# The residual of the first output projection in chunks, the third feed-forward product read early, and the first transposes of prompt attention between its scores

## What is computed

```python
yp = yp + jnp.concatenate([mix_p, att_p], axis=-1) @ w_out[i]
f_p, c_p = conv_ffn(rmsnorm(yp, g_ffn[i]), zeros, w_up[i], conv_w[i], conv_b[i], w_down[i])

def conv_ffn(h, prev, w_up, conv_w, conv_b, w_down):
    u = h @ w_up
    ext = jnp.concatenate([prev, u], axis=1)
    y = conv_b + sum(conv_w[k] * ext[:, k:k + l] for k in range(CONV_WIDTH))
    a, v = jnp.split(y, 2, axis=-1)
    return (jax.nn.silu(a) * v) @ w_down, ext[:, -(CONV_WIDTH - 1):]
```

## Time and profile before

| | us |
|---|---|
| median of 3 runs | 3093.95 (3091.4 to 3095.31) |
| the profiled execution, its own time | 3097.18 |
| its span, first to last instruction | 3095.1 |
| mean granted TensorE clock | 0.975 of full |
| PE busy in the span | 2953.5 |

### The profile page before, as it was taken

One profiled execution on the slowest core, in us unless ns is written; L12 is line 12 of the kernel. 1 busy time (PEld: TensorE's weight loads), 2 busy tenths in 40 slices (PEclk: granted clock), 3 DMA queues, 4 the chain that ended last, 5 costly groups with the idle time before them and its releaser, 6 DMA issues. The chain is left out here.

```text
span 3095.1 us, 51036 instructions
## 1 busy us (share of the span) xinstructions
PE 2953.5 (95%) x19316; PEld 2727.1 (88%) x19316; DVE 1572.5 (51%) x3486; ACT 814.9 (26%) x1506; POOL 954.3 (31%) x420
## 2 busy tenths in 40 slices
PE   8998979999989999999999999899999999999998
PEld 7996956666667799999999999897899999999998
DVE  6212147777545516652643726396247626526262
ACT  5002026767633303320211202114123202102020
POOL 4430000000000133444444443460344444444443
PEclk9999979999989999999999999999999999999999
DMA  6117730000257331111111111313111111111112
GB/s 185 52 40 241 248 141 2 1 2 1 77 162 229 99 113 46 41 38 51 41 41 48 38 51 38 117 53 118 41 53 35 40 48 47 38 51 36 52 36 89
DMA packets 128571, 222.76 MB, mean 72 GB/s; under 512 B 16006, under 2 KB 92140, under 8 KB 127232
## 3 DMA queue, kind: packets, MB, share of 16 engines
q1 hardware_dynamic: 108436, 201.57, 20.0%
q10 hardware_dynamic: 19980, 19.14, 2.3%
HBM read 202.61 MB, written 22.18 MB: 73 GB/s over the span
## 5 line engine op out<-in xcount | busy, mean ns | idle before, releaser
L382 POOL TENSOR_SCALAR weights_high<-weights_whole 128x1024 fp32r<-128x1024 f32 (+2 forms) x168 | 434.7, 2588 | 1065.9 <-PE banks L417 894.1
L413 PE MATMUL banks<-ffn_in_high,weights_high 128*128 128x364 f32 (+1 forms) x2112 | 468.5, 330 | 16.9 <-DVE ffn_in_low L280 9.2
L415 PE MATMUL banks<-ffn_in_low,weights_high 128*128 128x364 f32 (+1 forms) x2112 | 468.2, 330 | 0.0
L417 PE MATMUL banks<-ffn_in_high,weights_low 128*128 128x364 f32 (+1 forms) x2112 | 466.6, 329 | 0.0
L413 PEld LDWEIGHTS banks<-ffn_in_high,weights_high 128*128 128x128 f32 x2112 | 367.3, 189 | 18.9 <-issue 18.9
L2749 DVE SCALAR_TENSOR_TENSOR conv_out<-conv_ext,conv_w,conv_out 128x1024 f32<-128x1024 f32 x176 | 322.0, 1829 | 109.7 <-ACT conv_out L2685 94.9
L384 POOL TENSOR_TENSOR weights_low<-weights_whole,weights_high 128x1024 fp32r<-128x1024 f32 (+2 forms) x168 | 367.2, 2186 | 24.7 <-issue 0.2
L417 PEld LDWEIGHTS banks<-ffn_in_high,weights_low 128*128 128x128 f32 x2112 | 368.8, 189 | 0.0
L415 PEld LDWEIGHTS banks<-ffn_in_low,weights_high 128*128 128x128 f32 x2112 | 368.4, 189 | 0.0
L2777 DVE TENSOR_TENSOR x<-x,banks 128x728 f32 (+1 forms) x128 | 86.5, 718 | 386.9 <-PE banks L417 386.9
L2685 ACT ACTIVATE conv_out<-conv_ext,conv_b,conv_w 128x1024 f32<-128x1024 f32 (+1 forms) x176 | 138.3, 834 | 542.6 <-DVEq L2740 542.4
(11 more groups left out here) (431 smaller groups left out, 4618.7 us busy)
## 6 DMA issues: line engine op xcount, KB each, us to landing
weights_whole<-in_w_up SPq DMA_DIRECT2D x88, 512.0 KB, 3.5
past_rows<-in_kv_pages SPq DMA_DIRECT2D x160, 128.0 KB, 2.3
z<-in_kv_pages SPq DMA_DIRECT2D x96, 128.0 KB, 2.4
weights_whole<-in_w_down SPq DMA_DIRECT2D x32, 384.0 KB, 3.1
weights_whole<-in_w_down SPq DMA_DIRECT2D x32, 320.0 KB, 2.9
x<-in_cmp_pages ACTq DMA_DIRECT2D x64, 128.0 KB, 5.8
x<-in_cmp_pages SPq DMA_DIRECT2D x64, 128.0 KB, 5.6
cmp_rows<-in_cmp_pages ACTq DMA_DIRECT2D x64, 128.0 KB, 5.3
```

Of the source, the lines that this page charges most:

```text
L382: pool.tensor_scalar(high, whole, 1.0, None, ALU.mult)
L413: pe.matmul(o, wh, high[:, at], start=kk == 0, stop=False)
L415: pe.matmul(o, wh, low[:, at], start=False, stop=False)
L417: last = pe.matmul(o, wl, high[:, at], start=False, stop=kk == len(terms) - 1)
```

## The change

Three edits, and the order of the instructions behind them.

1. `project`, only where there is a residual to load: each of the eight chunks has a semaphore and a transfer of its own (546 KB). SP issues chunks 0 and 1 when each is split, then weight tiles 2 and 3, then chunks 2 to 7, then the other tiles. DVE waits for chunk m before it takes product m, and its loop is written out.
2. `conv_ffn`: DVE takes product 2 (gate half of pair 1) right after the taps of the gate half of pair 0. Pair 1 is written out too, so that the loop of the first part starts at pair 2.
3. `prompt_attention`: the last three score phases of period 1 move behind the first transposes, and the scores of period 2 close up behind them; DVE weighs units 0 and 1 one after the other ahead of these phases; ACT's exponentials of units 3 and 4 start with the fifth copy instead of the first.

```diff
--- before.py
+++ after.py
@@ -431,21 +431,28 @@ project
-        late_loaded = k.sem(ctx, "late_loaded")
+        late_loaded = [k.sem(ctx, f"late_loaded{m}") for m in range(n)] if late_load else []
...
-            def late():
-                if late_load:
-                    tokens.wait_ready(sp)
-                    sp.dma_start(late_load[0][:], late_load[1].rearrange("k p t -> p k t")).then_inc(late_loaded, 16)
-            if w.fetched:
-                late()
+            def late(first, end):
+                for m in range(first, end):
+                    tokens.wait_chunk(sp, m)
+                    sp.dma_start(late_load[0][:, m, :], late_load[1][m]).then_inc(late_loaded[m], 16)
+            if late_load:
+                late(0, 2)
+                for s in range(2):
+                    w.load(sp, 2 + s, s, w_src[2 + s], cols)
+                late(2, n)
+                with sp.Fori(2, n // 2) as j:
+                    for s in range(2):
+                        w.load(sp, j * 2 + s, s, w_src[j * 2 + s], cols)
+            elif w.fetched:
                 rest_of_pairs(sp, n, lambda m, j, s: w.load(sp, m, s, w_src[m], cols), w.fetched)
...
@@ -483,13 +490,16 @@ project, VectorE
-            if late_load:
-                dve.wait_ge(late_loaded, 16)
...
-            pairs(dve, n, take)
+            if late_load:
+                for m in range(n):
+                    dve.wait_ge(late_loaded[m], 16)
+                    take(m, m // 2, m % 2)
+            else:
+                pairs(dve, n, take)
@@ -1212,6 +1223,9 @@ prompt_attention (AHEAD = 3)
         starts = [0] + [2 * ((ends[2 * p + 1] - 1) // 2) - 1 for p in range(NP)]
+        for f in range(AHEAD, PHASES):
+            places.setdefault(f - AHEAD, []).append((1, f))
+        starts[0] = PHASES - AHEAD
         for p in range(NP - 2):
@@ -1303,9 +1317,8 @@ prompt_attention, TensorE
-            for p in range(2):
-                for f in range(PHASES):
-                    score(p, f)
+            for p, f in [(0, f) for f in range(PHASES)] + [(1, f) for f in range(AHEAD)]:
+                score(p, f)
@@ -1420,12 +1433,12 @@ prompt_attention, VectorE
-            for f in range(3):
+            for f in range(AHEAD):
                 phase(1, f)
-            weigh(0)
-            for f in range(3, PHASES):
+            for u in range(2):
+                weigh(u)
+            for f in range(AHEAD, PHASES):
                 phase(1, f)
-            weigh(1)
@@ -1501,7 +1514,9 @@ prompt_attention, ScalarE
-                    for x in range(total * r // count, total * (r + 1) // count):
+                    later = 0 if p else 4
+                    first, end = (total * max(0, y - later) // (count - later) for y in (r, r + 1))
+                    for x in range(first, end):
                         ahead[x // STEPS](x % STEPS)
@@ -2724,18 +2739,22 @@ conv_ffn, VectorE
+            def take(t, av):
+                w.wait_product(dve, t)
+                for dst, src, r in pieces(av):
+                    last = dve.tensor_tensor(dst, src, r, ALU.mult)
+                last.then_inc(taken, 1)
+
             def convolve(p, m, base):
-                first = p == 0 and isinstance(m, int)
+                first = p == 0 and isinstance(m, int) and m == 0
+                second = p == 0 and isinstance(m, int) and m == 1
...
-                    if not first:
-                        w.wait_product(dve, m * 2 + (base + av))
-                        for dst, src, r in pieces(av):
-                            last = dve.tensor_tensor(dst, src, r, ALU.mult)
-                        last.then_inc(taken, 1)
+                    if not first and not (second and av == 0):
+                        take(m * 2 + (base + av), av)
...
                     if av == 0:
                         last.then_inc(convolved, 1)
+                        if first:
+                            take(base + 2, 0)
...
-            convolve(0, 0, 0)
-            finish(0, 0)
+            for m in range(2):
+                convolve(0, m, 0)
+                finish(0, m)
             for p, n in enumerate(PARTS):
-                with dve.Fori(1, n) as m:
+                with dve.Fori(1 if p else 2, n) as m:
```

3 lines of the change are left out of this document (2 added, 1 removed).

## The result

| | before | with the change |
|---|---|---|
| median, first comparison | 3090.18 (3082.21 to 3095.31, 6 runs) | 3066.9 (3061.91 to 3071.37, 6 runs) |
| median, second comparison | 3090.07 (3086.36 to 3097.34, 23 runs) | 3070.66 (3063.22 to 3076.54, 6 runs) |
| the profiled execution | 3097.18, span 3095.1 | 3065.29, span 3063.1 |
| mean granted TensorE clock in it | 0.975 | 0.982 |

The change makes the kernel faster: the ratio is 0.992, 95% interval 0.9901 to 0.9939, and 0.9932 (0.9918 to 0.9945) the second time, thus 19 to 23 us. The forecast was 3074.4 with a range from 3068 to 3085: the sign and the places were right, the time was 1.1 us under the range in the first comparison and inside it in the second. The two profiled spans differ by 32.0 us, more than the comparisons give, so a part of that difference is not the change; the stages tell which.

A forecast was written before the change was run, and what follows sets the result against it. TensorE, busy 2953.5 of 3095.1 us, was taken as the bound. Projection 8.5, feed-forwards 8.6 and attention 2.5 sum to 19.6 us, taken from the median 3093.95: forecast 3074.4, range 3068 to 3085.

The forecast's parts named there:

- Bound, places, order: Whole kernel: TensorE bounds it, stalls at four places can go, and PE's earlier start there is an earlier end.
- Projection: First output projection: PE's 5.6 us wait for weight tile 2 and 2.9 us of low clock go, gain 8.5.
- The margin of tile 2: Projection: tile 2 lands about 2 us before it is needed, its split ends 6.7 us before PE wants it.
- Feed-forward: Fifth product of each layer: stall of 5.6 us removed, 1.3 comes back, net gain 4.3 a layer, 8.6 for both.
- But product 5 needs product 3 read: Feed-forward: PE waits at worst 1.6 us at product 5; 0.8 counted, plus 0.5 for clock and product 6.
- a loop's entry: Feed-forward: the first state copy took 1.88 us instead of 0.17 on entering the loop; writing out pair 1 might remove it.
- its gate half is as late as before and no later: Feed-forward, pair 1: it begins with the state copy instead of the reads, so its gate half keeps its lateness.
- the stall's 5.6 us: Feed-forward, fifth product: 4.04 us lost around the wait plus 1.6 in slow groups after it, for each layer.
- Attention: Start of prompt attention: the transposes of 468.66 start at 466.2, gain 2.5 us, bounds −1 and 4.
- From there the orders agree, and PE, not DVE, opens the next period, so the 2.5 stay: Attention after period 1: the 2.5 us gained at the start are kept.
- rival (b): Attention: DVE becomes the one waited for, the clock stays low, 2.5 becomes −1, total 3078; chance 0.12.
- Rival (d): Feed-forward: DVE becomes the bound through longer loop passes, the kernel gets slower, 3105 at 5.2 us a pass; chance 0.03.

The follow-up runs named there:

- with both tiles ahead: All three edits, but the projection's residual goes in one transfer behind weight tiles 2 and 3; the projection stage takes 103.47 us.
- behind all eight chunks: Kernel before with the residual in eight chunks, all issued ahead of weight tiles 2 and 3; the projection stage takes 102.47 us.
- One read more: All three edits, with the early read of product 2 done twice in each layer; feed-forward 0 takes 805.72 us, layer 1 801.08.
- Edit 3 alone: Kernel before with only the change of prompt_attention; 3089.8 us, ratio 1.0 (0.9991 to 1.001).
- the whole once more: The changed kernel, unchanged, measured again against the kernel before; 19.4 us less than before.
- In four pieces: All three edits with product 2 read twice, and GpSimd's split of every up weight tile in four 256-column pieces; feed-forward 0 takes 802.4 us.

## Why the prediction was off

**Bound, places, order.** Right. The stalls of the earlier trace rows are gone, PE starts the next product when the last ends, and the time stays gained to the end.

**Projection.** Forecast 8.5, measured 8.2 between the two profiles shown and 7.2 between the means (ten profiles with the edit, 102.0 to 103.3, and five without, 109.4 to 110.7). The mechanism is right; the term is 1.3 too large because the profile before had more low clock behind the wait than the others, 6.2 us where they had 3.2 to 4.7. The margin of tile 2 was enough: with the change and with both tiles ahead POOL waited for PE, and even behind all eight chunks its split was done some 2 us early.

**Feed-forward.** Forecast 4.3 a layer, measured 6.5 and 7.1 between the means (five profiles without the edit, split untouched: 808.1 and 802.0; seven with it and no more work of VectorE: 801.6 and 794.95). The step that failed is the one after "But product 5 needs product 3 read": I took half of a delay of 1.6 us, and 0.5 for clock, as coming back. Nothing came back. I had read 1.88 us as a loop's entry and 2.43 as something that straight code has too; both are VectorE held up while GpSimd splits a tile. So "its gate half is as late as before and no later" failed too. Counted from the stage's first matmul, product 3 is read after 62.8 us where it was 65.9: of the 3.1 us, 1.7 are the hold of the state copy and 0.6 that of `gated_low`, which both fall away. With the edit the reads of product 2 go in ahead, and the step under the next L384 is the copy at 1222.20, which delays nothing: VectorE has to wait for ScalarE's last tap there anyway, 2.75 us before and 0.54 now. One read more puts `gated_low` under the split instead, and the margin of about 1 us turns into a wait of 3.5. The rule that I named beside it, of the Trainium skill ("Runtime: NRT & Kernel Launch", Instruction fetch mechanics), that a taken branch off the resident pages costs a fetch, is not shown by these rows: the 1.88 us that seemed to agree with it stood there without a branch. What lies above the stall's 5.6 us is clock: layer 1 has a low stretch of 3.4 us that starts between 3028 and 3042 us in each profile without the edit and in none with it. Why is open. Edit 3 alone and the whole once more, in windows:

```profile
3030.00:3060.00 30.00, 27.95 (x159) 27.95 (x160) 5.38 (x8) 0.00 (x0) 15.32 (x10) 0.94 0.33 112
```

```profile
3030.00:3060.00 30.00, 30.00 (x183) 30.00 (x182) 5.41 (x8) 0.00 (x0) 13.50 (x8) 1.00 0.41 148
```

**Attention.** Forecast 2.5 that stay. The start gained 3.2 on average (2.4 between the two profiles shown), by the chain I had followed: the last score of the period comes 44.0 us after the first, forecast 43.9. "From there the orders agree, and PE, not DVE, opens the next period, so the 2.5 stay" failed: 2.1 us went back through the clock of the next 200 us, and the comparison of edit 3 alone has a ratio of 1.0. In its size that is rival (b) by half, but not by its mechanism: the clock of the start rose (0.68 after 0.64) and fell later.

**Sum and level.** By stages the change is worth 7.2 + 6.5 + 7.1 + 1.1 = 21.9 us; forecast 19.6. That the two are only 2.3 apart is partly luck: projection and attention were 2.7 too large together, the feed-forwards 5.0 too small. The other part of the miss is what it was taken from: the first three runs have a median of 3093.95, all comparisons since have 3088.9 to 3092.6 and the largest, 23 runs, 3090.07. From 3090.1, 21.9 less is 3068.2; the two medians lie at 3066.9 and 3070.66. I gave scatter 2 us, where the runs of one kernel spread over 7 to 13.

**Rival (d)** (VectorE as the bound) has nothing for it: its waits for PE keep the 4.4 us each (162.9 in 37).

## What to carry over

Before an odd duration is given a cause, lay the other engines' rows of the same microseconds beside it: a step that ends when another engine's instruction ends is held up by it. A reordering that removes a wait also decides which instruction stands under the other engine's work next; room of 1 us is not room. And cut every profile at the same landmarks: stages repeat within a few tenths or differ by whole low-clock stretches, where medians of whole runs need tens of runs.

## What the runs showed of the hardware

- A VectorE instruction on two SBUF operands, or a copy between SBUF tiles, that started during the subtraction of GpSimd's split (L384) lasted until that ended (2.43 us for 0.28, 1.86 for 0.17), or its own length longer (2.70 for 1.30); reads of the banks (1.41 us) did not. Under the first half (L382) such an add was held for less (1.05 for 0.28) or not at all (1.28). In four pieces the longest delay in pairs 0 and 1 was 0.5 us.
- An execution's clock differs from the next one's in the same place with the same instructions: 0.94 and 0.69 of full over 30 us in two executions of the changed kernel, 237.1 and 242.8 us for the stage.
- Eight transfers of 546 KB were all issued within 11.83 us as the chunks became free, and a tile issued behind them landed 7.2 us later; behind the one large transfer POOL was released 14.9 us after SP had issued that (1087.04 and 1101.89).
